# Seven-product FFN on one Trainium2 core: one weight sum per step, and products issued two at a time on two PSUM banks

## The reference

```
def swiglu(x, w_gate, w_up, w_down):
    return (jax.nn.silu(x @ w_gate) * (x @ w_up)) @ w_down

hdn = rmsnorm(x, gains[0])
x = x + 0.5 * rmsnorm(swiglu(hdn, ffn_w_gate[layer, 0], ffn_w_up[layer, 0], ffn_w_down[layer, 0]), gains[1])
```

## Time and profile before

| what | value |
|---|---|
| median of 3 runs | 2627.71 us (2626.11 to 2627.72) |
| the profiled execution | 2626.2 us; its span 2624.6 us |
| TensorE busy | 2493.1 us, 95% of the span, 19669 matmuls |
| VectorE busy | 1655.9 us, 63% |
| ScalarE busy | 1065.3 us, 41% |
| GpSimd busy | 410.7 us, 16% |
| mean granted TensorE clock | 0.989 of full |
| the four product stages | 208.1, 208.7, 209.2 and 211.5 us, 6048 matmuls |

### The profile page before, as it was taken

How to read it: one execution, slowest core, us unless ns; L and a number is a source line. 1 busy time by engine, 2 the same in 40 slices (tenths; PEclk the granted TensorE clock), 3 DMA queues, 4 the chain that set the end, 5 groups by cost and what they waited for, 6 DMA issues and landing times. The chain is left out here.

```text
span 2624.6 us, 50609 instructions
## 1 busy us (share of the span) xinstructions
PE 2493.1 (95%) x19669; PEld 2346.4 (89%) x19669; DVE 1655.9 (63%) x2874; ACT 1065.3 (41%) x2026; POOL 410.7 (16%) x601
## 2 busy tenths in 40 slices
PE   8999999998999989999998999999989989999998
PEld 7899999995557989999998999999979969899998
DVE  6888525546664688862588872467546666888723
ACT  4444324114443444442444442334354444444422
POOL 0000003023331200000200000255245532000001
PEclk9999999999999999999999999999999999999999
DMA  4233422248994123342123343223210133233431
GB/s 115 81 97 97 113 81 73 76 131 295 305 304 153 58 73 97 97 116 86 50 72 97 97 112 87 65 71 84 66 35 1 34 105 97 74 87 97 111 88 46
DMA packets 397837, 264.15 MB, mean 101 GB/s; under 512 B 10984, under 2 KB 370613, under 8 KB 397608
## 3 DMA queue, kind: packets, MB, share of 16 engines
q1 hardware_dynamic: 386096, 223.03, 30.1%
q0 software_dynamic: 11536, 38.28, 4.4%
HBM read 251.71 MB, written 9.56 MB: 100 GB/s over the span
## 5 line engine op out<-in xcount | busy, mean ns | idle before, releaser
L763 PE MATMUL ps<-x_part_hi,part_hi 128*128 128x272 f32 x2016 | 593.5, 294 | 43.0 <-DVE scratch L981 22.8
L763 PE MATMUL ps<-x_part_hi,part_lo 128*128 128x272 f32 x2016 | 584.2, 290 | 0.0
L763 PE MATMUL ps<-x_part_lo,part_hi 128*128 128x272 f32 x2016 | 581.9, 289 | 0.0
L507 DVE TENSOR_TENSOR w_lo<-w_raw,w_hi 128x1024 fp32r<-128x1024 f32 (+1 forms) x170 | 245.8, 1446 | 490.0 <-ACT w_hi L500 487.8
L500 ACT CAST w_hi<-w_raw 128x1024 fp32r<-128x1024 f32 (+1 forms) x170 | 199.0, 1170 | 641.8 <-PE ps L535 582.6
L763 PEld LDWEIGHTS ps<-x_part_hi,part_hi 128*128 128x128 f32 x2016 | 380.5, 189 | 59.8 <-DVE scratch L981 33.3
L763 PEld LDWEIGHTS ps<-x_part_lo,part_hi 128*128 128x128 f32 x2016 | 381.3, 189 | 0.0
L763 PEld LDWEIGHTS ps<-x_part_hi,part_lo 128*128 128x128 f32 x2016 | 380.4, 189 | 0.0
L1479 POOL TENSOR_TENSOR xT<-xT,rstd_rows 128x272 f32<-128x272 f32 x96 | 84.5, 910 | 1687.3 <-DVE rstd_rows L1504 1687.3
L535 PE MATMUL ps<-hd_hi,w_hi 128*128 128x272 f32 x1408 | 294.2, 290 | 4.4 <-DVE w_lo L507 4.3
L535 PE MATMUL ps<-hd_lo,w_hi 128*128 128x272 f32 x1408 | 291.6, 289 | 0.0
(11 more groups left out here) (575 smaller groups left out, 4473.3 us busy)
## 6 DMA issues: line engine op xcount, KB each, us to landing
w_raw<-in_ffn_w_down_dram SPq DMA_DIRECT2D x64, 704.0 KB, 4.5
w_pair<-in_ffn_w_gate_dram SPq DMA_DIRECT2D x72, 512.0 KB, 4.1
w_pair<-in_ffn_w_up_dram SPq DMA_DIRECT2D x72, 512.0 KB, 5.1
v_pages<-in_cache_a_v_dram POOLq DMA_DIRECT2D x128, 256.0 KB, 4.4
w_raw<-in_c_w_in_dram SPq DMA_DIRECT2D x33, 512.0 KB, 4.0
k_pages<-in_cache_a_k_dram SPq DMA_DIRECT2D x64, 256.0 KB, 4.3
k_pages_raw<-in_cache_a_k_dram SPq DMA_DIRECT2D x64, 256.0 KB, 4.2
w_raw<-in_ab_w_in_dram SPq DMA_DIRECT2D x25, 512.0 KB, 3.9
```

Of the source, the lines that this page charges most:

```text
L507: e.tensor_tensor(w_lo[:, n % 2, 0:nk * P], raw[:, n % RAW, 0:nk * P], w_hi[:, n % 2, 0:nk * P].bitcast(F32), ALU.subtract).then_inc(sem(" ...
L763: mm = e.matmul(ps[:, bank, 0:TH], w[:, k * P:(k + 1) * P], x[:, k, :], start=idx < 4 and k == 0 and w is wh and x is xp_hi[idx], stop=k = ...
```

## The change

- **Two products in turn.** From q = 7 on, products (q, q+1), q odd, are issued together: for each row tile and each high/low combination one matmul of q, then one of q+1, on two banks. All that either waits for is waited for ahead of both. As 7 is odd, for odd p the couples are (0,1) (2,3) (4,5) and product 6 goes with product 0 of the next p; for even p they are (1,2) (3,4) (5,6). The first seven products stay single, and so does the last.
- **Weight sums one per step.** For pair P: t4 is done in the step in which part 7P+3 is made (q = 7P-2), t3, t2 and t1 in the steps of parts 4, 5 and 6 of pair P-1 (q = 7P-8, 7P-7, 7P-6), thus well ahead of the parts that read them.
- **Normalised x.** Scalar makes x times gain (`xg`, sixteen activations of 272), Vector multiplies by rstd in four tensor_tensor of 1088.
- **LATE = 6 in place of 10**, so `pair_low` and `pair_high` are left for one hidden pair of tiles only (p = 2) and sixteen tiles in place of twelve are split late, near the end of the products and in the first down unit. A fourth x part (EARLY = 4) has a home that is free early.
- **Small moves.** low(0..3) go to p = 3 (idx 1, 2, 4, 5), x_part 6 to q = 2 on Vector and into the opening on Scalar, gate(3), up(3), hidden(3) and silu(3), high(3) one step later.

```diff
-LATE = 10
+LATE = 6
+EARLY = 4
...
+        def sum_due(q, what):
+
+            if q < RING:
+                pair = {"t4": 0, "t3": 1, "t2": 1, "t1": 1}[what]
+                return pair if q == ("t4", "t3", "t2", "t1").index(what) else None
+            p, idx = (q + RING) // PROD, (q + RING) % PROD
+            pair = p if what == "t4" else p + 1
+            return pair if idx == 3 + ("t4", "t3", "t2", "t1").index(what) and pair < WP else None
...
+        def pe_products(e, g, together):
+            par = last_slot(g)
+            for q in together:
+                pe_product_ready(e, g, q)
             for k in range(KH):
-                for w, x in ((wh, xp_hi[idx]), (wh, xp_lo[idx]), (wl, xp_hi[idx])):
-                    mm = e.matmul(ps[:, bank, 0:TH], w[:, k * P:(k + 1) * P], x[:, k, :],
-                                  start=idx < 4 and k == 0 and w is wh and x is xp_hi[idx],
-                                  stop=k == KH - 1 and w is wl, skip_group_check=idx >= 4)
-            mm.then_inc(sem("product_done"), 1)
+                for w_part, x_part in ((ring_hi, xp_hi), (ring_hi, xp_lo), (ring_lo, xp_hi)):
+                    for q in together:
+                        idx = q % PROD
+                        bank = 4 * (q // PROD % 2) + PRODUCTS[idx][1]
+                        opens = idx < 4 and k == 0 and w_part is ring_hi and x_part is xp_hi
+                        closes = k == KH - 1 and w_part is ring_lo
+                        mm = e.matmul(ps[:, bank, 0:TH], w_part[par][slot_of[q]][:, k * P:(k + 1) * P], x_part[idx][:, k, :],
+                                      start=opens, stop=closes, skip_group_check=idx >= 4)
+                        if closes:
+                            mm.then_inc(sem("product_done"), 1)
...
-            for q in range(PROD * WP):
-                pe_product(e, g, q)
+            for q in range(PROD):
+                pe_products(e, g, (q,))
+            for q in range(PROD, PROD * WP, 2):
+                pe_products(e, g, (q, q + 1) if q + 1 < PROD * WP else (q,))
...
+            def xg(n):
+                part, h, k0, negative = X_NORMED[n]
+                for k in range(k0, k0 + KH):
+                    of = neg_gains[:, KH * f + k - KH:KH * f + k - KH + 1] if negative else gain(l, n_pre, k)
+                    ins = e.activation(x_sums[:, part, k - k0, :], xT[:, k, half(h)], ACT.Copy, scale=of)
+                ins.then_inc(sem("ffn_scalar"), did("scalar", "xg", n))
...
-            low(0)
-            low(1)
-            dve_part(e, g, 0)
             dve_t3(e, g, 0)
             dve_t2(e, g, 0)
-            dve_part(e, g, 1)
+            dve_part(e, g, 0)
             dve_t1(e, g, 0)
...
                 if q + RING < PROD * WP:
                     dve_part(e, g, q + RING)
-                    if (q + RING) % PROD == 0:
-                        dve_t3(e, g, (q + RING) // PROD)
-                        dve_t2(e, g, (q + RING) // PROD)
-                    if (q + RING) % PROD == 1:
-                        dve_t1(e, g, (q + RING) // PROD)
-                    if (q + RING) % PROD == 3:
-                        dve_t4(e, g, (q + RING) // PROD)
+                if sum_due(q, "t4") is not None:
+                    dve_t4(e, g, sum_due(q, "t4"))
+                if sum_due(q, "t3") is not None:
+                    dve_t3(e, g, sum_due(q, "t3"))
+                if sum_due(q, "t2") is not None:
+                    dve_t2(e, g, sum_due(q, "t2"))
+                if sum_due(q, "t1") is not None:
+                    dve_t1(e, g, sum_due(q, "t1"))
```

More of the change, by code:

```diff
@@ L614, in vector_steps @@
-            steps += [("gate", 1), ("up", 1), *(("x_sum", n) for n in range(4)), ("hidden", 1), *(("x_part", n) for n in range(3))]
-            steps += [("gate", 2), ("up", 2), ("hidden", 2), ("low", 0), ("low", 1), ("part", 0), ("t3", 0), ("t2", 0), ("part", 1)]
-            steps += [("t1", 0), ("part", 2), ("x_part", 3), ("part", 3), ("t4", 0), ("x_part", 4), ("part", 4), ("x_part", 5)]
+            steps = [("gate", 0), ("up", 0), ("xn", 0), ("xn", 1), ("hidden", 0), ("xn", 2), ("xn", 3), ("gate", 1), ("up", 1)]
@@ L617, in vector_steps @@
+            steps += [*(("x_sum", n) for n in range(4)), ("hidden", 1), *(("x_part", n) for n in range(3)), ("gate", 2), ("up", 2)]
+            steps += [("x_part", 3), ("hidden", 2), ("t3", 0), ("t2", 0), ("part", 0), ("t1", 0), ("part", 1), ("part", 2), ("part", 3)]
+            steps += [("x_part", 4), ("part", 4), ("x_part", 5)]
             for q in range(PROD * WP):
                 p, idx = q // PROD, q % PROD
+                prev = STD - 1 + p // 2
                 steps += [(x, p) for x in {1: ("u_sum",), 2: ("w_sum",), 3: ("quarter",), 6: ("sums",)}.get(idx, ())]
-                prev = STD - 1 + p // 2
@@ L621, in vector_steps @@
                 steps += [("gated", prev)] * (idx == 0 and p % 2 == 0 and p > 0)
                 steps += [("pair_low", prev)] * (idx == 2 and p % 2 == 0 and p > 0 and prev < LATE // 2)
[L623 to L627, removed]
+                steps += [("x_part", 6)] * (q == 2) + [("part", q + RING)] * (q + RING < PROD * WP)
@@ L628, in vector_steps @@
+                steps += [(x, sum_due(q, x)) for x in ("t4", "t3", "t2", "t1") if sum_due(q, x) is not None]
+                steps += {4: [("gate", 3), ("up", 3)], 6: [("hidden", 3)]}.get(q, [])
+                steps += [("low", {1: 0, 2: 1, 4: 2, 5: 3}.get(idx))] * (p == 3 and idx in (1, 2, 4, 5))
                 steps += [("late", x) for x in late_at(q) if q < PROD * WP - 1]
-            return steps + [("gated", KU - 1)] + [("late", x) for x in range(7, KF - LATE)]
+            return steps + [("gated", KU - 1)] + [("late", x) for x in range(9, KF - LATE)]
@@ L631, in scalar_steps @@
         def scalar_steps():
-            steps = [("silu", 0), ("x_part", 0), ("high", 0), ("silu", 1), ("x_part", 1), ("x_part", 2), ("high", 1), ("silu", 2)]
-            steps += [("high", 2), ("part", 0), ("part", 1), ("part", 2), ("x_part", 3), ("part", 3), ("x_part", 4)]
-            steps += [("part", 4), ("x_part", 5)]
+            steps = [*(("xg", x) for x in range(4)), ("silu", 0), ("x_part", 0), ("high", 0), ("silu", 1), ("x_part", 1), ("x_part", 2)]
+            steps += [("x_part", 3), ("high", 1), ("silu", 2), ("high", 2), *(("part", n) for n in range(4)), ("x_part", 4)]
@@ L636, in scalar_steps @@
+            steps += [("part", 4), ("x_part", 5), ("x_part", 6)]
             for q in range(PROD * WP):
@@ L642, in scalar_steps @@
                 steps += [("part", q + RING)] * (q + RING < PROD * WP)
-                steps += [("x_part", 6)] * (q == 0) + [("silu", 3)] * (q == 4) + [("high", 3)] * (q == 6)
+                steps += [("silu", 3)] * (q == 5) + [("high", 3)] * (q == 7)
                 steps += [("late", x) for x in late_at(q)]
-            return steps + [("late", x) for x in range(9, KF - LATE)]
+            return steps + [("late", x) for x in range(11, KF - LATE)]
         def plain_gate(j):
@@ L892, in act_gate_up @@
             act_split(e, first + 6, 0, KD)
-            act_x_part(e, g, 1)
-            act_x_part(e, g, 2)
+            for n in (1, 2, 3):
+                act_x_part(e, g, n)
             high(1)
@@ L947, in act_gate_up @@
             act_split(e, first + 4 * STD + 1, 0, KU)
-            for x in range(9, KF - LATE):
+            for x in range(11, KF - LATE):
                 act_late(e, f, x)
@@ L1015, in low, with xn @@
                                 ALU.subtract).then_inc(sem("ffn_vector"), did("vector", "low", j))
[L1017 to L1026, removed]
+            def xn(n):
+                part, h, _, _ = X_NORMED[n]
+                wait_step(e, "scalar", f, "xg", n)
+                e.tensor_tensor(x_sums[:, part, :, :], x_sums[:, part, :, :], rb[:, half(h)].unsqueeze(1).to_broadcast([P, KH, TH]),
+                                ALU.mult).then_inc(sem("ffn_vector"), did("vector", "xn", n))
             dve_rstd_x(e, s, first + 2)
@@ L1100, in dve_gate_up @@
             dve_gated(e, f, KU - 1)
-            for x in (7, 8):
+            for x in (9, 10):
                 dve_late(e, f, x)
             dve_split(e, first + 4 * STD + 1, 0, KU)
-            for x in range(9, KF - LATE):
+            for x in range(11, KF - LATE):
                 dve_late(e, f, x)
```

72 lines of the change are left out of this document (39 added, 33 removed).

## The result

The changed kernel takes 2797.5 us (median of 4 runs, 2794.7 to 2802.8) against 2627.7: ratio 1.065, 95% interval 1.063 to 1.067. It is slower by 170 us; 112 were forecast.

A forecast was written before the change was run, and what follows sets the result against it. It took TensorE's products as the bound, with at most 66 us of waits from Vector's order to win. 2626.2 - 66 + 160 (stalls) + 20 (clock) - 3 (banks) + 1 (down entry) = 2738 us; own range 2705 to 2765, widened to 2695 to 2775.

The forecast's parts named there:

- the bound: Product stages: of 74.3 us beyond matmul time, 66 lie in waits made by Vector's order; most would go with single products.
- the two waits: Couple (4,5) of odd p stalls 2.1 us for w_sum, couple (5',6') of even p 1.4 us for quarter; some stalls longer.
- their chain: Steps from a product seen done to TensorE's start: 5.05 us before w_sum, 7.34 us before quarter, mostly Vector's queue.
- The DMA of w_pair: Load for t3, wanted 5 steps after release, 8 before the change; 8 us left against landing of 3.7 to 7.7: nothing.
- the entry into down: Start of the down projection: less time for Vector's split in three FFNs, 2 us hidden in the last; +1 us in all.
- The head: Normalised x there: less Vector work, some 7 us more on Scalar; worth nothing, up to 1 us per FFN if a cast came late.
- The term of 14 falls: TensorE's clock in product stalls: a fifth of 28 and half of 16 stalls followed by falls, 1.5 us each, +20 us.
- the opening: First products of each FFN: waits of 1.5 + 1.4 + 1.6 = 4.5 us, as much as before.
- (a): Vector is caught up at both product waits, so they cost their least: 2610 us, faster; chance 0.06.
- (c): Product matmuls alternating banks pay more than L535 shows, up to 74 us, half felt: 2704 us; chance 0.05.
- (d): Weight sums come late: t3 is up before w_pair has landed and Vector waits; 34 us more, 2772 us; chance 0.04.
- (b): Clock in product stalls: no falls give 2718 us, all 2784; none or nearly all beyond the forecast's range, chance 0.07.

## Why the prediction was right and where it was wrong

**Right: the bound, the two waits, and their chain.** The loss is where it was put, w_sum for odd p and quarter for even p, 36 and 35 waits, seven w_sum stalls per FFN within 0.16 us of each other. The chain of Vector's instructions took 4.97 us where 4.99 were walked. Taking the sums out of it moved the stalls to the 1.1 and 1.0 us expected. The DMA of w_pair and the entry into down cost what they were put at (nothing, 1 us). The head was put at nothing and cost one wait of 1.55 us in the first FFN, over the 1 us per FFN given for a late cast.

**Wrong by size: the clock.** The term of 14 falls, +20 us, should have been 38 falls and 57 us, +54.6 against before. The price of one was right (1.5 put, 1.4 to 1.5 measured); the count was not. This is the largest single miss, 35 us; with the stalls below it makes the product windows 253 us each where some 230 were forecast. Of the 28 stalls of w_sum put at 2.1 us a fifth was to be followed by a fall, and 20 were; of the 16 longer ones half, and 14 were; the opening was left out, and 4 begin there. I took a fifth because none of the twelve quarter waits of 1.7 us idle (1.9 by starts) in the kernel before had been followed by one. In the changed kernel none of 26 stalls of 1.4 to 1.7 us was followed by a fall, 21 of 29 of 2.2 to 2.5 were, and 16 of 19 above 2.5. The 0.2 us by which the stalls came out longer than walked does not explain the count: over ten of the kernels (all but the one with needless matmuls) 11 of 20 stalls of 2.0 to 2.15 us, most of them in the opening, were followed by a fall, and 15 of 24 of 2.2 us in the kernel with the waits asked for last, so a fifth was too low at 2.1 us as well. The range was too narrow on its own terms: it was cut at 2775, while the case in which all 44 fall stood at 2784 and both upper ends together above 2820.

**Wrong by size: the stalls.** Stalls and distances were to give 94 - 3 = +91 and gave +120. Of the 29 us, 20 are stalls, 180 us in place of 160: some 14 are the restart, 0.26 us where I took 0.06 from a single product, 68 times; some 4 the opening (5.4 us per FFN in place of 4.5); the rest is in p = 2 to 5 (3.1, 3.5, 4.1 and 2.9 in place of 2.6, 3.2, 3.9 and 2.6, restart included) and 17. The other 9 are what did not go. The 66 us that Vector's order was said to make in the kernel before were 53 of stalls; 3 were matmuls at the low clock, and 10 were distances a little above 126.2 ns (127.8 in the mean). The stalls went and the distances shortened by 7 us: together 60 in place of the 66 + 3 put down. A slip without weight: the paired matmuls are 5664, not 5712, as the last product is single.

**The rivals.** (a), Vector caught up at both waits, did not come: the stalls are four times its 0.57. (c) is out by the 125.0 ns. (d), a late w_pair, is out: no matmul waits for its DMA, and of Vector's sums two do, 1.9 us in all, each just before a product stage begins. (b) was the right one to price at more: "all fall" stood at 2784, with a chance of 0.07 that it shared with "none", and the measured time lies beyond it by less than the 29 us by which the stalls were mis-sized. That changing banks would make the clock fall by itself is not borne out: with couples (0,1) and (2,3) in every p and no long wait behind them 4 falls begin in the stages, as many as with single products, and with all couples and the gaps filled 4 as well.

## What to carry to other kernels

Before issuing two chained steps in turn, write down for each wait how many independent steps remain between producer and user; a distance that drops to zero puts the other engine's whole queue, not one instruction, into the path. Put what the other engine may do later (here t1 and t2) behind the instruction that someone waits for. And where stalls of TensorE are as long as those after which its clock was seen to fall (here 2 us and more), price the fall with the stall: here a third of the loss was the clock, and needless matmuls in the gap got 48 us back.

## What the runs showed of the hardware

- In the product stages of ten of the kernels (all but the one with needless matmuls) none of 341 stalls of TensorE of 0.33 to 1.9 us was followed by a fall of the granted clock, 129 of 172 of 2.0 us and more were, and no fall began without such a stall. Each fall to 1.2 GHz cost 1.4 to 1.5 us. That filling part of the gap keeps the clock up is shown by the kernel with needless matmuls (38 falls to 4).
- Couples that alternate two banks with other weights each time took 125.0 ns a matmul of 272 columns where they waited for nothing, single products on one bank 126.1. Over all four stages the means were 126.6 in the changed kernel and 126.7 in the single one, and couple (0,1) took 125.7 where single products stood around it, so little of the difference is left in a kernel.
- After a wait on w_sum or quarter TensorE began 0.06 us (single products; 0.10 in the opening) or 0.26 us (couples) after Vector's row ended; asking for that wait last made it 0.15 for both.
